# Rotating the cached rotary keys on GpSimd, token by token, instead of by a swap product on TensorE

## The reference, cut to what matters

```
k = concat(latent @ w_uk, krope)            # 64 + 32 values a head
k = rmsnorm(k, g_qk_k)
k_rope = rope(k[64:96], position)           # x1*cos - x2*sin, x2*cos + x1*sin
score = q_nope . k_nope + q_rope . k_rope
```

## Time and profile before

| | us |
|---|---|
| median of 3 runs | 1328.42 (1321.75 to 1332.19) |
| time of the profiled execution | 1320.99 |
| its span, first to last instruction | 1319.3 |
| PE busy | 1237.7 (94%) |
| DVE busy | 816.2 (62%) |
| ACT busy | 509.3 (39%) |
| POOL busy | 191.7 (15%) |

### The profile page before, as it was taken

The page is one execution under the profiler, slowest core; times in us unless marked ns, Lnnn a source line. Parts: engine busy times, 40 slices in busy tenths (PEclk is TensorE's granted clock), DMA queues, the critical chain, the costliest instruction groups (busy, mean ns, idle before and its releaser), DMA issues.

```text
span 1319.3 us, 24253 instructions
## 1 busy us (share of the span) xinstructions
PE 1237.7 (94%) x9344; PEld 1103.1 (84%) x9344; DVE 816.2 (62%) x1392; ACT 509.3 (39%) x908; POOL 191.7 (15%) x337
## 2 busy tenths in 40 slices
PE   4998989988999899999999899899899998999998
PEld 4985767767989599999999677677699977999998
DVE  5566685767574577664556666757756556766442
ACT  4231322434343355553332324233443424655331
POOL 1234343320000000000012534224100000000000
PEclk8999999998999899999999899899899998999999
DMA  8624565571457845554565257557445784555552
GB/s 327 237 55 147 168 185 172 171 253 65 160 196 302 364 136 185 188 173 183 192 239 200 67 170 229 149 153 216 168 159 192 286 319 193 175 177 192 178 175 96
DMA packets 75090, 250.42 MB, mean 190 GB/s; under 512 B 11440, under 2 KB 44544, under 8 KB 54368
## 3 DMA queue, kind: packets, MB, share of 16 engines
q1 hardware_dynamic: 58896, 194.05, 41.8%
q0 software_dynamic: 13968, 47.57, 11.1%
q10 hardware_dynamic: 2112, 7.26, 1.4%
HBM read 241.60 MB, written 7.46 MB: 189 GB/s over the span
## 4 chain that ended last, share of the span: by engine, by line
PE 76%; DVE 9%; DMA 5%; issue 4%; ACT 3%; PEld 1%; POOLq 0%; POOL 0%; DVEq 0%; ACTq 0%; PEldq 0%
PE ps L1427 48%; PE ps L1436 18%; DMA ring<-in_units 3%; PE ps L1703 2%; DMA big<-in_pages 2%; DVE ring_r L745 2%; PE ps L1860 1%; PEld ps L1427 1%; DVE ssn L1071 1%; DVE xg_r L761 1%; DMA xT<-in_xt 1%; PE ps L1662 1%; PE ps L1663 1%; PE ps L1715 1%; ACT big_r L437 1%
## 5 line engine op out<-in xcount | busy, mean ns | idle before, releaser
L1436 PE MATMUL ps<-wuq_b,latT 128*128 128x260 f32 x1024 | 252.7, 396 | 13.7 <-ACT sc L437 11.7
L1427 PE MATMUL ps<-qkA_r,ring_r 128*128 128x264 f32 x880 | 252.7, 287 | 0.0
L1436 PEld LDWEIGHTS ps<-wuq_b,latT 128*128 128x128 f32 x1024 | 192.6, 194 | 59.0 <-issue 13.3
L365 POOL DMA_DIRECT2D big<-in_pages x256 | 138.7, 542 | 216.8 <-issue 200.9
L1427 PEld LDWEIGHTS ps<-qkA_r,ring_r 128*128 128x128 f32 x880 | 168.8, 192 | 0.0
L1427 PE MATMUL ps<-big_r,ring_r 128*128 128x264 f32 x512 | 145.5, 284 | 0.0
L745 DVE TENSOR_TENSOR ring_r<-ring,latT_r 128x2048 fp32r<-128x2048 f32 x42 | 96.2, 2292 | 60.4 <-ACT latT_r L437 59.5
L437 ACT ACTIVATE latT_r<-ring 128x2048 fp32r<-128x2048 f32 x42 | 80.4, 1915 | 108.3 <-DMA ring<-in_units 108.3
L437 ACT ACTIVATE qkA<-ps 128x512 f32<-128x512 f32 x86 | 51.0, 593 | 163.2 <-PE ps L1436 163.1
L1427 PE MATMUL ps<-xg_r,latT_r 128*128 128x264 f32 (+1 forms) x384 | 110.7, 288 | 0.0
L1427 PE MATMUL ps<-qkA_r,latT_r 128*128 128x264 f32 x320 | 94.5, 295 | 15.3 <-DVE xg_r L761 15.0
(11 more groups left out here) (370 smaller groups left out, 2945.8 us busy)
## 6 DMA issues: line engine op xcount, KB each, us to landing
ring<-in_units SPq DMA_DIRECT2D x136, 1024.0 KB, 4.9
big<-in_pages POOLq DMA_DIRECT2D x256, 144.0 KB, 3.4
latT<-in_pages SPq DMA_DIRECT2D x256, 128.0 KB, 2.7
big<-in_units SPq DMA_DIRECT2D x16, 1024.0 KB, 11.7
mat<-in_mats POOLq DMA_DIRECT2D x2, 2048.0 KB, 11.2
xg<-in_memt POOLq DMA_DIRECT2D x2, 1024.0 KB, 6.9
out_mk<-latT ACTq DMA_DIRECT2D x2, 1024.0 KB, 3.9
out_mv<-latT ACTq DMA_DIRECT2D x2, 1024.0 KB, 6.4
```

What stands on the lines that cost most here:

```text
L365: pool.dma_start(lat[:, s, pg, :], pages[bass.ds(at_page[pg] * DEPTH + l, 1), :, 256:544] .rearrange("a p n -> p (a n)")).then_inc(lat_in[ ...
L1427: ins = mm(out, a(i, k), b(j, k), start=first and k + n == 0, stop=last and k == KD - 1 and n == 2)
L1436: ins = mm(out, a, b, start=i == 0, stop=i == len(pairs) - 1)
```

## The change

GpSimd now rotates the keys while their tokens lie on partitions (`rotate(b)`), straight from the page buffer into `krN`, with five elementwise operations: 512 elements a partition, then four of 256. Its tables of cosine and sine are turned to that layout in layer 0 (eight transposes and two copies) and multiplied in each layer by the norm's weight (`kr_tables`). PE then transposes the rotated keys and DVE only copies them out (`kr_ready`). The swap product, its scaling, and DVE's three operations at n = 6 are gone, and so is ACT's copy. PE's transposes wait for `kr_rot`, which POOL now raises. In POOL's queue the page load of sequence 1 and `rotate(0)` now stand ahead of the pooling mixer, and each later `rotate(b)` stands behind the maximum of sequence b - 1 and ahead of the load of sequence b + 1.

```diff
-POOL_STEPS = 16
+POOL_STEPS = 16 + 4 * B
...
+        kr_cos, kr_sin, kr_part = within(qkB_f, 512, PAGES, ROPE), within(qkA_f, 1216, PAGES, ROPE), within(qkA_f, 1728, PAGES, ROPE // 2)
...
+                def rotate(b):
+
+                    wait_ge(lat_in[b % 2], 16 * PAGES * (l * (B // 2) + b // 2 + 1))
+                    if l + b:
+                        wait_ge(sems["kr_ready"], l * B + b)
+                    kr, half = lat[:, b % 2, :, 256:288], ROPE // 2
+                    step(pool.tensor_tensor(krN[:, :, :], kr, kr_cos, ALU.mult))
+                    step(pool.tensor_tensor(kr_part, kr[:, :, half:], kr_sin[:, :, 0:half], ALU.mult))
+                    step(pool.tensor_tensor(krN[:, :, 0:half], krN[:, :, 0:half], kr_part, ALU.add))
+                    step(pool.tensor_tensor(kr_part, kr[:, :, 0:half], kr_sin[:, :, half:], ALU.mult))
+                    pool.tensor_tensor(krN[:, :, half:], krN[:, :, half:], kr_part, ALU.add).then_inc(sems["kr_rot"], 1)
+
+                wait_ge(sems["lat_used"], at["lat_used"].free())
+                load(page_numbers(mybir.EngineType.Pool, PAGES), 1, range(PAGES))
+                wait_ge(sems["kr_tables"], l + 1)
+                rotate(0)
                 wait_ge(layer_in, 64 * (l + 1))
...
-                    wait_ge(sems["lat_used"], at["lat_used"].free())
-                    load(page_numbers(mybir.EngineType.Pool, b * PAGES), b % 2, range(PAGES))
+                    if b > 1:
+                        wait_ge(sems["lat_used"], at["lat_used"].free())
+                        load(page_numbers(mybir.EngineType.Pool, b * PAGES), b % 2, range(PAGES))
                     maximum()
+                    rotate(b)
                 maximum()
...
-                            f(krN[:, :, :], lat[:, b % 2, :, 256:288], ACT.Copy)
...
+                    elif i in (3, 5) and l == 0:
+                        freed(v.tensor_copy(con[:, C_COS4 if i == 3 else C_SIN4:(C_COS4 if i == 3 else C_SIN4) + 512], tile()))
...
+                g_kr, half = gN[:, 1, :].unsqueeze(1).broadcast_to([P, PAGES, ROPE]), ROPE // 2
+                step(v.tensor_tensor(kr_cos, old_cos, g_kr, ALU.mult))
+                step(v.scalar_tensor_tensor(kr_sin[:, :, 0:half], old_sin[:, :, 0:half], -1.0, g_kr[:, :, half:], ALU.mult, ALU.mult))
+                step(v.tensor_tensor(kr_sin[:, :, half:], old_sin[:, :, half:], g_kr[:, :, 0:half], ALU.mult))
+                tell("kr_tables")
...
-                            freed(v.tensor_scalar(krC[:, :, :], tile().rearrange("p (g n) -> p g n", g=4), gain[:, G_KR4:G_KR4 + 1], None, ALU.mult))
-                            tell("kr_scaled")
+                            freed(v.tensor_copy(krS[:, :, :], tile().rearrange("p (g n) -> p g n", g=4)))
+                            tell("kr_ready")
...
-                            step(v.tensor_tensor(krS[:, :, :], krC[:, :, :], con[:, C_COS4:C_COS4 + 512].rearrange("p (g n) -> p g n", g=4), ALU.mult))
                             wait("kr_sq")
-                            v.tensor_reduce(ssr[:, :], krQ[:, :, :], AXX, ALU.add)
-                            freed(v.tensor_tensor(krC[:, :, :], tile().rearrange("p (g n) -> p g n", g=4),
-                                                  con[:, C_SIN4:C_SIN4 + 512].rearrange("p (g n) -> p g n", g=4), ALU.mult))
-                            step(v.tensor_tensor(krS[:, :, :], krS[:, :, :], krC[:, :, :], ALU.add))
-                            tell("kr_rot")
+                            step(v.tensor_reduce(ssr[:, :], krQ[:, :, :], AXX, ALU.add))
...
                         if n == 5:
-                            wait("kr_sq")
+                            wait("kr_rot")
...
-                        if n == 6:
-                            wait("kr_scaled")
-                            ready(product(bank(), [(swap4, krC[:, :, :])]))
```

More of the change, by code:

```diff
@@ L92 @@
     gate_in=0, gate_la=0, gate_dec=0, qbd_ready=0, att_ready=0, gvs_ready=0, gst_ready=0, gla_state=0, gla_raw=0, mix_side=0,
-    kr_scaled=0, kr_rot=0, dec_max=0, dec_in=0, dec_sum=0, olat_ready=0, km_raw=0, km_stat=0, km_ready=0,
+    kr_tables=0, kr_rot=0, kr_ready=0, dec_max=0, dec_in=0, dec_sum=0, olat_ready=0, km_raw=0, km_stat=0, km_ready=0,
     xq_raw=0, xq_stat=0, xk_ready=0, xv_sum=0, head_out=0, x_in=0, x_p=0, x_t=0, hot_q=0, xs_in=0, hot_p=0, xs_out=0, xo_ready=0,
@@ L213, in decoder @@
         psq = [qkA_f[:, 0:512], qkA_f[:, 512:1024], qkB_f[:, 1536:2048]]
-        krS, krC = within(qkB_f, 0, 4, PG), within(qkB_f, 512, 4, PG)
+        krS = within(qkB_f, 0, 4, PG)
+        kr_cos, kr_sin, kr_part = within(qkB_f, 512, PAGES, ROPE), within(qkA_f, 1216, PAGES, ROPE), within(qkA_f, 1728, PAGES, ROPE // 2)
+        gN = within(m, 264, 2, ROPE)
+        old_cos, old_sin = within(con, C_COS4, PAGES, ROPE), within(con, C_SIN4, PAGES, ROPE)
         wa, wb = within(mix_f, 0, 2, 400), within(mix_f, 4 * T, 2, 400)
@@ L863, in _ @@
                     elif i == 9:
+                        step(v.tensor_scalar(gN[0:ROPE, 0, :], ident[0:ROPE, 0:ROPE], gain[0:ROPE, G_KR4:G_KR4 + 1], None, ALU.mult))
                         dve.wait_ge(layer_in, 64 * (l + 1))
@@ L898, in _ @@
                         tell("s_ready")
-                        freed(v.tensor_copy(gvs_n[:, :], tile()[0:B, 0:256]))
+                        t = tile()
+                        step(v.tensor_copy(gN[:, 1, :], t[:, 256:256 + ROPE]))
+                        freed(v.tensor_copy(gvs_n[:, :], t[0:B, 0:256]))
                         tell("gvs_ready")
@@ L1475, in sample @@
                         ready(mm(bank(), rep[0:QK, :], turns[0:QK, :, 0:TP], start=True, stop=True))
+                    elif i in (1, 2) and l == 0:
+                        t = bank()
+                        for g in range(4):
+                            o = (C_COS4 if i == 1 else C_SIN4) + P * g
+                            ins = nc.tensor.transpose(t[:, P * g:P * g + P], con[:, o:o + P], ident)
+                        ready(ins)
                     elif i == 3:
@@ L1505, in sample @@
                         for k in range(2):
-                            ins = nc.tensor.transpose(t[0:B, k * P:k * P + P], z[:, GV + k, TP:T], ident)
-                        ready(ins)
+                            nc.tensor.transpose(t[0:B, k * P:k * P + P], z[:, GV + k, TP:T], ident)
+                        ready(mm(t[:, 256:256 + ROPE], ones[0:ROPE, :], gN[0:ROPE, 0, :], start=True, stop=True))
                 normed_projection(U_IN, hi_in, 1, hi_in2, sample)
@@ L1711, in rotary @@
                     wait("rot_in")
-                    wait("kr_rot")
+                    wait("kr_ready")
                     t = bank()
```

## The result

| | before | changed |
|---|---|---|
| median | 1328.84 us (4 runs, 1321.75 to 1332.19) | 1534.88 us (4 runs, 1533.48 to 1536.23) |
| ratio | | 1.156, interval 1.151 to 1.161 |
| profiled span | 1319.3 | 1533.2 |
| mean granted clock | 0.974 | 0.902 |

What follows compares the result with a forecast made beforehand. PE mostly bounds the loop, in places DVE. Layer 0 79.1, layer 1 80.8, tables 1.2 and clock 14 give +175 us: 1496 on the profiled 1320.99, put at 1500 with half the median's 7 us difference; range 1450 to 1550.

Steps and rivals of the forecast that it cites:

- Switches: POOL's passages between elementwise operations and maximum: four before, 32 after; 7.8 us into elementwise, about 5.9 extra into the maximum.
- Rival 1: POOL's code switches nearly free once both codes have been used: about -20 us, 1301 or 1308 us; chance 0.07.
- rival 4: POOL's switch before each maximum starts early, during the wait; with 3 us hidden each, 1455 us; chance 0.04.
- rival 2: Both POOL switches cost 5.9 us; chain 17.3 instead of 19.2 us, total 1470 us; chance 0.12.
- The chain of 19.2 us: DVE's local maxima to rotated keys on POOL: 6.2 + 0.4 maximum + 7.8 switch + 4.8 rotation.
- PE's stand: PE idle 8 to 14 us before each sequence's transposes; 85.8 us more waiting in layer 0, 86.3 in layer 1.
- Transposes to the next local maxima, with the clock: Six passages a layer, each 1.5 us shorter from saved work; lower granted clock adds 1.0 us a sequence, 14 us total.
- The upper bound of 3.5 us a sequence: Most that PE's half clock could cost each of 14 sequences, from granted clock 0.87 over 27 us; 1.0 taken.
- the sum: Layer 0 79.1, layer 1 80.8, tables 1.2 and clock 14: +175 us.
- the two stretches behind the 1.0: Loop at 807 to 834: 4.1 us standing, clock 0.87; at 159 to 185: 3.75 us stand, clock 1.00.
- Sequence 0: First sequence of each layer: rotation ready at 106.3 in layer 0; later by 3.3 us there, 4.5 in layer 1.
- Gains: Swap product and DVE operations removed: 9 us a layer over six passages, plus 1 in the last sequence.

Runs made afterwards that it cites:

- the run without switches: Changed kernel with each maximum over the partitions replaced by a GpSimd copy, rotation kept on GpSimd: 1341.5 us, ratio 1.011.
- its control: Kernel before the change with each maximum over the partitions replaced by a GpSimd copy: 1321.5 us, ratio 0.997.

## Why the prediction was right

The forecast was 1500 (1450 to 1550), slower by over 1% at 0.92. Point by point:

- **Switches.** Right, and shown from two sides: with them out of the changed kernel's loop 7 to 20 us of loss are left, with them put into the kernel before it is 73. Predicted 7.8 us into the rotation, measured 7.6 on average (7.0 to 9.2). Predicted 6.2 from local maxima to the maximum; measured 6.0 to 6.6 in 12 of 16 sequences, 7.4 and 8.0 in sequence 5, where POOL still issued page DMAs when the input came, and 11.2 (372.55 to 383.74) and 8.5 in sequence 6. Rival 1 (nearly free once used) and rival 4 (early start) are out, rival 2 (5.9 us for each) as well. Rival 1's own figure, some 20 us below the kernel before, would not have come either: without switches the changed kernel is 7 to 18 us above it (1331.1 and 1341.5 against 1324.0). What a passage consists of inside GpSimd no trace shows; shown is that it depends on which kind of operation follows which.
- **The chain of 19.2 us.** Measured from DVE's local maxima to the transposes: 19.4, 19.6, 19.5, 19.2, 18.8, 19.8 and, behind the 11.2 us maximum, 24.8 us in layer 0. Sum 141.1 against 134.4; layer 1 has 139.5. The rotation took 1.25 + 4 x 0.73 + 4 x 0.18 = 4.9 us, up to 5.3 in sequences 0 and 7; I had taken 4.8.
- **PE's stand.** Its size was right, its place only in part. I had all of it at the transposes, 8 to 14 us each; the trace has 5.2 to 9.3 there and some 5 earlier in the same chain, at the pairs, while DVE stands for the maximum. The sequences came out longer than the 36 to 38 us (42 in one) forecast: 37.3 to 44.7.
- **Transposes to the next local maxima, with the clock.** This is the step that was mis-sized. I took 1.5 us off each passage for the work saved and put 1.0 on for the clock. Measured in layer 0, six passages: 20.1, 21.7, 21.7, 25.8, 17.5 and 19.5, together 126.3 us, against 111 without the clock in my sum: 2.5 us on each, not 1.0. The transposes' own 1.09 us instead of 0.60 show that PE starts each passage at half clock, and with the extra products, which keep it out of that, the same six passages take 111.8 us. From the mean clocks, 0.974 and 0.902, the time at half clock is 69 us of 1319 before and 300 us of 1533 after. The upper bound of 3.5 us a sequence, worked out from one stretch, held; the run with extra products puts at least 36 us on it where the sum had 14. My reading of the two stretches behind the 1.0 was uneven: by the same measure PE stood 4.1 us in one and 4.5 in the other (3.75 is only the longest single gap).
- **Sequence 0.** Transposes predicted at 106.3, measured 107.36. The next local maxima came 8.5 us later than before (129.89 against 121.39), where I had 3.3. Some 1.1 us of the difference are the later start, 2.2 the half clock (transposes 1.09 instead of 0.60, the pair behind them 3.67 instead of the 2.0 that I took). The third part is a term that I had put at nothing: the mixer's new place. POOL's elementwise operations now run beside an operation of DVE on the way to the local maxima. First the kernel before, then the changed one:

```profile
111.15 2.57 DVE L971 SCALAR_TENSOR_TENSOR area<-area,gain,y 128x256 f32<-128x256 f32 x5 [0.16 <-DVE ring L941]
...
117.31 4.91 DVE L1001 SCALAR_TENSOR_TENSOR area<-area,gain,y 128x256 f32<-128x256 f32 x5 [0.16 <-DVE ring L971]
...
119.04 1.42 POOL L426 TENSOR_TENSOR y<-y,con 128x528 f32<-128x528 f32 x1 [0.18 <-POOL y L423]
```

That is 2.3 us, and 2.8 in layer 1 (5.41 against 2.57). The three parts make 5.6, a little more than the 5.2 by which I missed. In the run with extra products the transposes take 0.63 us, the operation of DVE 5.70, and the first local maxima still come 7.7 us later than before, so the clock alone does not explain it.

- **Where the missing 39 us went.** The profiled spans differ by 213.9 us, the sum had 175. Over both layers the chains have 12 more than forecast, the six passages 19, sequence 0 10; the last sequence has 3 less. The largest part is the passages, the clock's term. That 1534.9 still lies in the range is owed in part to the range's width.
- **Gains.** I had 9 us a layer and 1 at its end, 20 in all; the kernel without swap and rotation shows 15, and 7.0 and 6.7 us in the six passages of its layers. So this was somewhat high, and it is a gain that exists only when the rotation costs nothing.
- **Not in the sum.** That the load's landing comes to lie in front of five POOL operations in sequences 6 and 7 (some 20 us in the run without switches) I had not looked for. In the changed kernel the switches take the time in which the pages land, so it does not come on top.

The Trainium skill, "GPSIMD Engine Reference", section 2.1, has the load of freshly called code at about 6 us with no visible instruction; the maximum's passage agrees, and the rotation's shows 1.6 us more here. Section 3.1 of the same page of the Trainium skill keeps elementwise work on VectorE; the runs agree where the work is well placed: put in place of the swap product, the five operations on GpSimd cost 20 us even without switches (1341.5 against 1321.5), on VectorE nothing (1325.1 against 1326.9). Badly placed they cost 88 on VectorE too (1411.9 against 1324.2).

## What to carry to other kernels

Before work is moved to an engine that looks idle, read the gaps in its timeline and the bare rows of its queue, and ask what the new neighbours in the queue will make of them: a passage that costs 7 us once a layer can cost 14 us in every turn of a loop. Work that only changes its place in that queue gets new neighbours on other engines too: the mixer's new place cost some 2.5 us a layer. A result should be produced as many steps ahead of its use as the consuming engine normally leads; the same 2.4 us of work cost 16 us over the run without rotation at a distance of three steps and 103 at one. The next use counts as well: at three steps' distance but with the copy one step ahead of the rotary scores it was 34. And a wait that makes TensorE stand in every turn costs twice, once as a stand and again in half clock behind it.

## What the runs showed of the hardware

- A GpSimd passage from elementwise operations to the maximum, or back, stands 6 to 9 us, each time, however recently the other code ran (32 passages in the changed kernel, one of them longer, see below). Copies pass freely between both: with five copies in place of the rotation, the later maxima start 0.3 us behind their input, or behind POOL's own last page DMA. The DMA queues show nothing of a passage: their instruction traffic was 75 packets and 1.23 MB on q8 with 4 of them and with 32.
- TensorE did more work in less time: 96 added products of 128x512 in the waits took 36 us off the kernel, with the granted clock up from 0.902 to 0.949.
- The passage into the maximum of sequence 6 took 11.2 us in layer 0 and 8.5 in layer 1, and 10.2 to 11.6 in the four other runs with both switches. Page DMAs directly ahead of it are not enough to explain it: the maximum of sequence 5 also stands directly behind 16 of them and comes 7.2 us behind their end. In sequence 6 the transfer of the memory tokens is on its way too; whether it lengthens the passage was not tried.
- VectorE's elementwise operations on two operands in SBUF get longer while GpSimd's run: the five of 128x256 above took 2.57 us in both layers of four runs in which no GpSimd operation ran beside them (the kernel before, its control, no rotation, rotation on VectorE with steps 3 and 6), and 3.73, 4.04, 4.91, 5.41 and 5.70 us with 1.9, 2.2, 3.4, 3.9 and 4.2 us of GpSimd's elementwise operations beside them. VectorE's copies of 128x512 out of PSUM and its sums kept their 0.69 us.
